# Weights packed in load order, tiles moved to 64-byte starts, and the position embedding as one more column of the compression matmuls

## What is computed

```python
starts = jnp.arange(n_cmp) * CMP_STRIDE          # 15 blocks, stride 16
win_idx = starts[:, None] + jnp.arange(CMP_BLOCK)[None, :]
def compress(t, j):                              # j = 0 keys, 1 values
    blk = t[:, win_idx] + pe[j][None, None, :, None, :]
    h = jax.nn.silu(jnp.einsum('bnlgd,ldf->bngf', blk, w1[j]))
    return h @ w2[j]
```

## Time and profile before

| | |
|---|---|
| median of 3 runs | 2589.13 us |
| the profiled execution | 2592.49 us, of which the span from first to last instruction is 2590.70 us |
| mean granted TensorE clock over the span | 0.948 of full speed |
| busy: PE, DVE, ACT | 2344.5, 1672.1, 1098.6 us |
| DMA | 531.24 MB in 293659 packets, 208080 of them under 2 KB; mean 205 GB/s |

### The profile page before, as it was taken

How to read it: one execution, slowest core, us unless ns; L and a number is a source line. 1 busy time by engine, 2 the same in 40 slices (tenths; PEclk the granted TensorE clock), 3 DMA queues, 4 the chain that set the end, 5 groups by cost and what they waited for, 6 DMA issues and landing times.

```text
span 2590.7 us, 30688 instructions
## 1 busy us (share of the span) xinstructions
PE 2344.5 (90%) x11132; PEld 1926.3 (74%) x11132; DVE 1672.1 (65%) x2111; ACT 1098.6 (42%) x1221; POOL 0.2 (0%) x4
## 2 busy tenths in 40 slices
PE   0999994899999985999999898999999989899998
PEld 0787884688788774788788686778878869677786
DVE  7677667676677776676677644577757764456444
ACT  1434634433534554443433434543444343464333
POOL 0000000000000000000000000000000000000000
PEclk9999997999999995999999987999999998799999
DMA  9787431497488540596588632248758883223552
GB/s 376 273 299 280 142 109 33 160 322 264 173 321 311 185 163 16 203 321 235 211 319 301 186 115 82 98 166 322 281 187 306 307 239 107 98 98 114 178 194 105
DMA packets 293659, 531.24 MB, mean 205 GB/s; under 512 B 14800, under 2 KB 208080, under 8 KB 275024
## 3 DMA queue, kind: packets, MB, share of 16 engines
q1 hardware_dynamic: 293584, 530.23, 58.9%
HBM read 529.12 MB, written 1.05 MB: 205 GB/s over the span
## 4 chain that ended last, share of the span: by engine, by line
PE 80%; DVE 10%; ACT 5%; issue 2%; DMA 2%; SPq 1%; DVEq 0%; ACTq 0%
PE GU L1391 14%; PE GU L1393 14%; PE GU L1395 14%; PE PY L1391 9%; PE PY L1393 9%; PE PY L1395 9%; DVE wL L810 2%; ACT wH L490 2%; PE TM L1441 1%; PE PY L1409 1%; PE PY L1693 1%; PE PY L1591 1%; PE PY L1688 1%; DMA M<-in_ada_t 1%; DVE M L817 1%
## 5 line engine op out<-in xcount | busy, mean ns | idle before, releaser
L810 DVE TENSOR_TENSOR wL<-raw,wH 128x2048 fp32r<-128x2048 f32 x352 | 794.6, 2279 | 331.0 <-ACT wH L490 330.5
L490 ACT ACTIVATE wH<-raw 128x2048 fp32r<-128x2048 f32 x352 | 659.3, 1899 | 216.9 <-PE PY L1395 101.7
L1391 PE MATMUL GU<-wH,xH 128*128 128x512 f32 (+1 forms) x1600 | 642.3, 401 | 35.0 <-DVE xL L898 16.7
L1393 PE MATMUL GU<-wL,xH 128*128 128x512 f32 (+1 forms) x1600 | 631.2, 394 | 0.0
L1395 PE MATMUL GU<-wH,xL 128*128 128x512 f32 (+1 forms) x1600 | 630.7, 394 | 0.0
L1391 PEld LDWEIGHTS GU<-wH,xH 128*128 128x128 f32 x1600 | 302.3, 189 | 107.3 <-issue 35.9
L553 ACT ACTIVATE hH<-TM 128x512 fp32r<-128x512 f32 x88 | 52.7, 599 | 715.7 <-PE TM L1441 715.7
L1395 PEld LDWEIGHTS GU<-wH,xL 128*128 128x128 f32 x1600 | 302.1, 189 | 71.6
L1393 PEld LDWEIGHTS GU<-wL,xH 128*128 128x128 f32 x1600 | 302.7, 189 | 65.8
L817 DVE CUSTOM_DVE_ANT_0 ada<-ada,cond 128x1024 f32<-128x1024 f32 x256 | 298.1, 1220 | 0.0
L1391 PE MATMUL PY<-wH,hH 128*128 128x512 f32 x704 | 224.2, 399 | 27.0 <-DVE hL L911 27.0
(11 more groups left out here) (278 smaller groups left out, 2074.6 us busy)
## 6 DMA issues: line engine op xcount, KB each, us to landing
ada<-in_ada_t SPq DMA_DIRECT2D x128, 1024.0 KB, 8.0
raw<-in_ffn_wi SPq DMA_DIRECT2D x176, 512.0 KB, 5.8
raw<-in_ffn_w_in SPq DMA_DIRECT2D x176, 512.0 KB, 5.6
raw<-in_ffn_wo SPq DMA_DIRECT2D x88, 512.0 KB, 4.4
raw<-in_ffn_w_out SPq DMA_DIRECT2D x88, 512.0 KB, 4.3
raw<-in_mix_w_in SPq DMA_DIRECT2D x64, 512.0 KB, 4.5
M<-in_ada_t SPq DMA_DIRECT2D x16, 1024.0 KB, 10.4
raw<-in_a_w_in SPq DMA_DIRECT2D x32, 512.0 KB, 4.5
```

The source lines that it names most:

```text
L490: act.activation(wH[:, slot, 0:words], raw[:, slot, 0:words], ACT.Copy).then_inc(s_high, 1)
L810: dve.tensor_tensor(wL[:, slot, 0:words], raw[:, slot, 0:words], wH[:, slot, 0:words], ALU.subtract).then_inc(s_split, 1)
L1391: pe.matmul(outs[i], aH, wh[i], start=first, stop=False)
L1393: pe.matmul(outs[i], aH, wl[i], start=False, stop=False)
```

## The change

The host lays out the weights: one array per use, in which the pieces stand one after the other in the order in which SP loads them, so that a partition's part of a half piece is one run of 4096 bytes (before: 4 runs of 1024 bytes in `load_up`, 2 of 2048 in `load`, one of 4096 in `load_down`). `w1_` becomes one DMA for keys and one for values with a run of 8192 bytes a partition, `ws_` one run of 4096. What is loaded, its order and its size in bytes stay, and so do all waits of SP. `acc` moves to the end of the tiles; `C_END` grows by 8 words, `hc_` by 4, and `M`, `w2_`, `hc_` follow `cst`, so that every tile of a kilobyte and more starts on a multiple of 64 bytes. `cT_` is laid out by token within the stride, with rows of 34 words (16 blocks of group 0, 16 of group 1, then two columns of `peT`), filled by four ACT copies of 64 x 256 and one small DVE copy; the compression is 16 matmuls of 33 adjoining columns for each j, whose column 32 is the embedding's product. Line 1693 goes.

```diff
-C_END = C_FREQ + 8
+C_END = C_FREQ + 16
...
-        acc = sb("acc", [P, 4])
         x = sb("x", [P, NT, D])
...
         cst = sb("cst", [P, C_END])
+        M = sb("M", [P, ARENA])
+        w2_ = sb("w2_", [P, 2, 64])
+        hc_ = sb("hc_", [P, 2, 32])
...
-        M = sb("M", [P, ARENA])
+        acc = sb("acc", [P, 4])
...
-            def load(view, k0, nk, lo, width):
+            def load(src, words=PIECE):
...
-                dst = raw[:, slot, 0:nk * width].rearrange("p (k n) -> p k n", k=nk)
-                for q in range(2):
-                    sp.dma_start(dst[:, q * nk // 2:(q + 1) * nk // 2, :],
-                                 view[:, k0 + q * nk // 2:k0 + (q + 1) * nk // 2, lo:lo + width]
-                                 ).then_inc(s_raw[slot], 16)
+                for g in range(2):
+                    half = slice(g * words // 2, (g + 1) * words // 2)
+                    sp.dma_start(raw[:, slot, half], src[:, half]).then_inc(s_raw[slot], 16)
...
+                load(T["up_w"][l, j // 2, q][bass.ds(c, 1)].rearrange("c p n -> p (c n)"))
...
+                load(T["down_w"][l, j // 2][bass.ds(c, 1)].rearrange("c p n -> p (c n)"))
+            def load_mixer(w, pieces):
+                at = 0
+                for k0, lo, width in pieces:
+                    load(w[:, at:at + 4 * width], 4 * width)
+                    at += 4 * width
...
                     for k in range(2):
-                        for two in range(2):
-                            sp.dma_start(w1_[k].rearrange("p (l f) -> p l f", f=P)[two * 64:(two + 1) * 64],
-                                         T["cmp_w1_2"][i, k].rearrange("(l two) d f -> two d l f", two=2)[two]
-                                         ).then_inc(s_w1, 16)
+                        sp.dma_start(w1_[k], T["cmp_w1"][i, k]).then_inc(s_w1, 16)
...
-                    sp.dma_start(ws_, T["gm_ws_2"][i].rearrange("g t s -> t g s")).then_inc(s_gm, 16)
+                    sp.dma_start(ws_, T["gm_ws"][i].rearrange("t (g s) -> t g s", s=P)).then_inc(s_gm, 16)
...
-                act.activation(dst[0:64], src[0:64], ACT.Copy)
-                act.activation(dst[64:P, :, 0:S - 1], src[64:P, :, 1:S], ACT.Copy).then_inc(s_aT, 1)
+                src = TMf.rearrange("p (j g q n two) -> p j two n g q", j=2, g=2, q=16, two=2)
+                for j in range(2):
+                    for two in range(2):
+                        r = slice(64 * two, 64 * two + 64)
+                        ins = act.activation(cT_[r, j, :, 0:32].rearrange("p n (g q) -> p n g q", g=2),
+                                             src[r, j, two], ACT.Copy)
+                ins.then_inc(s_aT, 1)
...
+                dve.tensor_copy(cT_[:, :, :, 32:34].rearrange("p j n h -> p j h n"),
+                                peT[:, (l - 2) * 32:(l - 1) * 32].rearrange("p (j h n) -> p j h n", j=2, h=2))
                 dve.tensor_copy(v2_[:, 0], GU[:, :, 384:512])
...
-                pe.wait_ge(s_w1, 80 * (l - 1))
+                pe.wait_ge(s_w1, 48 * (l - 1))
...
-                        pe.matmul(PY[:, 2, 64 * j:64 * j + 30], w, cT_[:, j, :, 2 * n:2 * n + 16 * (NCMP - 1) + 1:16],
-                                  start=(n == 0), stop=(n == 15))
-                    for n in range(16):
-                        w = w1_[j][:, n * P:(n + 1) * P]
-                        at = (l - 2) * 32 + j * 16 + n
-                        ins = pe.matmul(PY[:, 2, 64 * j + 32:64 * j + 33], w, peT[:, at:at + 1],
+                        ins = pe.matmul(PY[:, 2, 64 * j:64 * j + 33], w, cT_[:, j, n % 8, n // 8:n // 8 + 33],
                                         start=(n == 0), stop=(n == 15))
```

More of the change, by code:

```diff
@@ L63, with whole @@
 C_FREQ = C_CSIN + 32
-C_END = C_FREQ + 8
+C_END = C_FREQ + 16
 N_CONST = 2
 N_LATE = 6
+def whole(order, width=512):
+    return [(k0, lo, width) for lo in order for k0 in (0, 4)]
+PIECES_A = whole((2 * D, D, 0, 2 * D + 512, 3 * D, 3 * D + 512, D + 512, 512)) + [
+    (k0, 4 * D + lo, 512) for k0 in (0, 4) for lo in (0, 512)]
+PIECES_B = whole([h * 512 for h in range(6)]) + whole([3 * D + h * 512 for h in range(2)])
+C_IN, C_OUT = 4376, 4376 + D
+PIECES_C = (whole((512, 0)) + whole((1024,), 280) + whole((1816, 1304, 2328, 2840, 3352, 3864))
+            + [(k0, C_IN + h * 512, 512) for h in range(2) for k0 in (0, 4)]
+            + [(k0, C_OUT + h * 512, 512) for k0 in (0, 4) for h in range(2)])
 class Tally:
@@ L432, in _ @@
                     ffn(l, j)
[L433 to L448, removed]
+                elif l < 2:
+                    load_mixer(T["ab"[l] + "_w"], (PIECES_A, PIECES_B)[l])
                 else:
@@ L725, in nsa @@
                     chained(act.activation(pec[:, k:k + 1], PY[:, 2, 64 * k + 32:64 * k + 33], ACT.Copy))
-                    ins = act.activation(hc_[:, k, :], PY[:, 2, 64 * k:64 * k + 30], ACT.Silu, bias=pec[:, k:k + 1])
+                    ins = act.activation(hc_[:, k, 0:2 * NCMP].rearrange("p (g n) -> p g n", g=2),
+                                         PY[:, 2, 64 * k:64 * k + 32].rearrange("p (g n) -> p g n", g=2)[:, :, 0:NCMP],
+                                         ACT.Silu, bias=pec[:, k:k + 1])
                 ins.then_inc(s_hc, 1)
@@ L1862 @@
     given = {name: _np.ascontiguousarray(inputs[name]) for name in _INS}
-    both = lambda name: _np.concatenate([_np.asarray(inputs[name]), _np.asarray(inputs[name + "_2"])])
+    array = lambda name: _np.asarray(inputs[name])
+    both = lambda one, two: _np.concatenate([array(one), array(two)])
     given["vec_cols"] = _np.ascontiguousarray(_np.concatenate([_np.asarray(a).reshape(-1, P) for a in (
-        inputs["c"], inputs["c_2"], inputs["norm_g"], inputs["norm_g_2"], inputs["gm_bs_2"], both("ada_b"),
+        inputs["c"], inputs["c_2"], inputs["norm_g"], inputs["norm_g_2"], inputs["gm_bs_2"], both("ada_b", "ada_b_2"),
@@ L1871, with packed @@
     given["table"] = table()
+    def packed(w, pieces):
+        rows = w.reshape(ND, P, -1)
+        return _np.concatenate([rows[k0:k0 + 4, :, lo:lo + width].transpose(1, 0, 2).reshape(P, 4 * width)
+                                for k0, lo, width in pieces], axis=1)
+    given["up_w"] = _np.ascontiguousarray(both("ffn_wi", "ffn_w_in_2").reshape(4, 2, 2, 4, P, 2, NF, CF).transpose(
+        0, 1, 2, 6, 4, 3, 5, 7)).reshape(4, 2, 2, NF, P, PIECE)
+    given["down_w"] = _np.ascontiguousarray(both("ffn_wo", "ffn_w_out_2").reshape(4, 2, NF, 2, P, D).transpose(
+        0, 1, 2, 4, 3, 5)).reshape(4, 2, NF, P, PIECE)
@@ new lines @@
+    for name in "ab":
+        given[name + "_w"] = packed(_np.concatenate([array(name + "_w_in")[0], array(name + "_w_out")[0]], axis=1),
+                                    PIECES_A if name == "a" else PIECES_B)
+    given["c_w"] = _np.stack([packed(_np.concatenate(
+        [array("mix_w_in_2")[i], _np.concatenate([array("proj_a_2")[i], array("proj_b_2")[i]]), array("w_out_2")[i]],
+        axis=1), PIECES_C) for i in range(2)])
+    given["cmp_w1"] = _np.ascontiguousarray(array("cmp_w1_2").reshape(2, 2, 16, P, P).transpose(0, 1, 3, 2, 4)).reshape(
+        2, 2, P, PIECE)
@@ L1872 @@
+    given["gm_ws"] = _np.ascontiguousarray(array("gm_ws_2").transpose(0, 2, 1, 3)).reshape(2, P, D)
     for name, a in given.items():
```

49 lines of the change are left out of this document (6 added, 43 removed).

## The result

The changed kernel takes 2507.8 us (median of 4 runs, 2505.2 to 2512.5), the kernel before beside it 2589.5 us: ratio 0.968, 95% interval 0.9665 to 0.9704. Forecast were 2541.5 us within 2530 to 2560. The sign was right, the gain is 82 us where 47.6 were booked, and the time lies under the range. The profiled execution took 2505.53 us, its span is 2504.0 us, and the mean granted clock 0.955.

A forecast was written before the change was run, and what follows sets the result against it. TensorE was taken as the bound (80% of the chain), with DMA mattering only where PE waits on it. Gains of 26.7 + 18.9 + 2 = 47.6 us took the median from 2589.13 to 2541.5 us, range 2530 to 2560.

The forecast's parts named there:

- The bound, and the cover of DMA: FFN loops: TensorE is the bound and covers DMA, so 4 KB packets instead of 1 KB bring nothing there.
- The compression: Both c mixers: folding the embedding into the 33-column products is free and line 1693's time goes, 26.7 us in all.
- Rival 3: Behind the compression: PE finds something else not ready, half of the 26.7 us goes, 2555 us; chance 5%.
- The entry of mixer c: FFN ends before mixers c: longer packets land the first piece in time, shorter waits and less low clock, 18.9 us.
- Rival 2: Entry of mixers c: PE still waits for the loads, the 18.9 us stay, 2560 us; chance 6%.
- The start: First 65 us, bound by DMA: up pieces load faster with 8 KB runs, 2 us, ends 0 and 5.
- rival 4: Mixer b, phase (1,1): packed rows 128 KB apart in HBM slow 16 loads, kernel slower, 2594 us at 118 GB/s; chance 3%.
- Alignment: Matmul operands, FFN and `by_channel`: which operand is off 64 bytes makes no difference, so nothing was booked.
- Rival 1: All matmuls: alignment bounds each, 17 to 20 ns apiece at 512 columns, time 2400 to 2461 us; chance 5%.
- The sum: Whole kernel: 26.7 + 18.9 + 2 = 47.6 us gained, median 2541.5 us.

The follow-up runs named there:

- the load alone: The kernel before with only the packed weights and their load queue changed: 2572.8 us, ratio 0.992.
- The kernel with its tiles put back: The kernel after with its tile moves taken back, all else kept: 2543.1 us, ratio 0.981.

## Why the prediction was wrong

**The bound, and the cover of DMA** held: with the load alone the FFNs kept their time at 0.82 share, packets of 4 KB or not.

**The compression** held. The step without line 1693 costs 10.4 us alone, as written. In the kernel after it costs 9.6: more of it runs before the clock falls (1.00 of full speed over the first 3.78 us). So 13.9 us came off the chain in the first mixer (23.50 to 9.56) and 14.3 in the second (23.95 to 9.69), 28.2 against 26.7 in all. Rival 3 fell: the copies stayed in their cover. That a column is free next to 30 held too.

**The entry of mixer c** held in its mechanism and, in the load alone, to the hundredth (1.50 us, and 11.07 to the next product). In the kernel after the first mixer's wait is 1.89 us and the way to the next product 12.53 us instead of 11.08, the second's 1.54 and 11.18. The 1.45 us are low clock: the granted clock is 0.63 of full speed from 1425.4 to 1430.0 us. The kernel with its tiles put back has 1.50 and 11.07 us before both mixers c, so it may be the faster products that bring PE to this piece a little too early; that is not shown. There 16.9 us of the 18.9 came off: 8.10 + 6.44 of waits and 0.74 + 1.67 behind them. The first piece was cut at 1420.43 us, 5.0 us before the last down piece, where I had 7.0; ACT's copy needs 1.91, so the lateness fell into the room. The rate in the window was 383 GB/s, where I took 420. Rival 2 fell.

**The start**: the first product came 1.5 us sooner, 2 booked. That is no firm number: the first `hH` lies at 90.3 to 92.5 us in the four kernels with the old layout (mean 91.7) and at 85.7 to 90.8 in the ten with the new (mean 88.4), 3.2 us in the mean.

These three together come to 28.2 + 16.9 + 3.2 = 48.3 us beside the 47.6 of the forecast. That they meet so closely is in part luck: two terms were too small by 1.5 and 1.2 us and one too large by 2.0. The 19.5 us in the forecast's upper end are worked out nowhere, the text has 18.9; it changes nothing.

**Mixer b**: rival 4 fell; its stretch takes 207.7 us with the load alone, 208.8 before.

**Alignment** is the step that failed, a term put at nothing that measured 37 us: "Per column both are 0.456 ns: it makes no difference which operand is off, so I book nothing." The two rows were right and the inference wasn't. The rows 9 and 10 differ in columns as well as in roles, and both kinds of product had the same distance between their operands, 32 bytes: they compare nothing with an agreeing pair. Equal cost per column was chance: once the operands agree the one falls from 0.456 to 0.443 ns and the other rises to 0.468. Rows with an agreeing pair did not exist before, so the cost had to be bounded from both sides, by the method used for every other unseen term. The most that a product could give back stood in the text: 20 ns over 512 columns at 2.4 GHz. Half of that over the FFNs' 88 turns of 72 products is 63 us; booked as an end of the range, it would have held the result.

**Rival 1** looked in the right place and had a third of the size right: 6 ns of its 17 to 20. Its mechanism was half right: what counts is the distance of the two operands and not the 64-byte start that the change gave them. That the change met the distance was luck; with every tile on 64 bytes but 64 off, the gain is gone (2544.2 us). The Trainium skill, "TensorE: Matmul & The Clock Gate", section "Back-to-back issue gap", has 216 ns at 512 columns for isolated matmuls, and about 131 ns beside it for a sustained stream of weight loads and matmuls. The traces agree with neither: no run's mean came under 226.8 ns, 11 above the first. Where the 6 ns went shows against the kernel with its tiles put back, whose span of 2541.0 us is 37.0 above 2504.0: a full FFN turn takes 16.80 instead of 17.23 us, an FFN 4.1 less, 33 us over eight; mixer b's stretch gives 4, a and c next to none. The 4 us are the weak part: in two other kernels whose x tiles agree that stretch took 206.9 and 207.3 us, not 203.8, and no run says why.

**The sum** with this one term: 47.6 + 37 = 84.6 us, against 82 measured. The range failed because it took its upper end from the other terms alone.

## What to carry to other kernels

When PE runs a long stream of matmuls at full clock and each takes some 9% longer than its columns at the clock (233 against 213 ns), compare the SBUF addresses of stationary and moving tiles before anything larger: here a distance that 256 divides was worth 1.4% of the kernel, for one 16-byte tile declared elsewhere. Round the start of every matmul tile to 256 bytes, not 64: that gives the agreement whatever stands between. This was seen for float32r products of 512 columns; those of 256 columns lost 3 ns by it, so look at the pace of each form. And where a trace holds no instance of the state that an edit makes, bound the term from both sides, instead of booking it at nothing because two rows of the old state agree.

## What the runs showed of the hardware

- The pace of float32r products of 512 columns depends on the distance of their operands in the partition, counted by 256 bytes: 0.227 to 0.228 us at 0 (256 bytes off included), 0.233 at 32, 64 and 128, 0.234 at 96, 0.233 in a mixture of 144 and 16. The absolute start doesn't count (all tiles 32 bytes off: 2507 us).
- It is the same with DVE and ACT still (233.3 against 227.0 ns) and without a DMA packet (233.1 against 227.9): the cost isn't a collision with another engine or with the transfers.
- For 256 columns with the roles swapped it is the other way round: 0.120 us in agreement, 0.117 at 32, 0.118 at 64, 0.119 at 128. These are 384 products, 1 us in all. Both kinds of product take the same tiles, so one distance can't serve both; separate tiles weren't tried.
- The cost isn't that of single products: with `xL` alone 32 bytes off, the three products average 0.233, with 238 ns on the one during which `xL` is loaded.
- What in the chip makes this stays open. The last point suggests that the load of the next stationary tile and the reading of the moving one share the memory, but no run here separates the two reads.
